# A hybrid mLSTM and attention layer on one core: the token's norm scale moves from x to the products of the projections

## What is computed

```
def rmsnorm(x, g):
    y = xf * lax.rsqrt(jnp.mean(xf * xf, axis=-1, keepdims=True) + EPS)
    return (y * g.astype(jnp.float32)).astype(x.dtype)
...
h = rmsnorm(x, g_pre_mix[l])
proj = h @ w_in[l]
m_qk, m_v, m_o, m_if, a_q, a_k, a_v, merge = jnp.split(proj, IN_SPLITS, axis=-1)
m_qk = jax.nn.silu(causal_dwconv(m_qk, m_conv_w[l], m_conv_b[l]))
...
hm = mlstm_chunkwise(..., i_pre, jax.nn.log_sigmoid(f_pre))
y_m = (jax.nn.sigmoid(m_o) * hm) @ w_branch_m[l]
ha = diff_attention(a_q, a_k, a_v, lam)
g_m, g_a = jnp.split(jax.nn.sigmoid(merge), 2, axis=-1)
mix = (g_m * y_m + g_a * y_a) @ w_out[l]
```

## Time and profile before

| | us |
|---|---|
| median of 3 runs | 1852.43 |
| lowest, highest | 1851.65, 1852.64 |
| span of the profiled execution | 1850.7 |
| TensorE busy | 1836.6 |
| VectorE busy | 1116.1 |
| ScalarE busy | 899.2 |
| first product of the projections starts | 12.72 |

### The profile page before, as it was taken

How to read it: one execution, slowest core, us unless ns; L and a number is a source line. 1 busy time by engine, 2 the same in 40 slices (tenths; PEclk the granted TensorE clock), 3 DMA queues, 4 the chain that set the end, 5 groups by cost and what they waited for, 6 DMA issues and landing times.

```text
span 1850.7 us, 35627 instructions
## 1 busy us (share of the span) xinstructions
PE 1836.6 (99%) x13864; PEld 1745.0 (94%) x13864; DVE 1116.1 (60%) x1340; ACT 899.2 (49%) x1174; POOL 66.6 (4%) x92
## 2 busy tenths in 40 slices
PE   8999999999999999999999999999999999999998
PEld 8999999999999999999999889999999999988886
DVE  6666556645665566545555557766667667755555
ACT  6554445444454455444434446555555555544443
POOL 2800000000000000000000000000000000000000
PEclk9999999999999999999999999999999999999999
DMA  7665666566656665666666754666666666665554
GB/s 241 194 192 175 191 182 177 177 188 181 178 172 192 179 176 177 188 193 193 192 192 196 253 198 149 194 193 194 193 193 193 192 194 190 196 215 193 194 193 143
DMA packets 164514, 351.44 MB, mean 190 GB/s; under 512 B 10937, under 2 KB 11473, under 8 KB 163793
## 3 DMA queue, kind: packets, MB, share of 16 engines
q1 hardware_dynamic: 162784, 344.11, 61.1%
q10 hardware_dynamic: 1280, 5.08, 0.7%
q0 software_dynamic: 368, 1.09, 0.2%
HBM read 348.12 MB, written 2.12 MB: 189 GB/s over the span
## 4 chain that ended last, share of the span: by engine, by line
PE 97%; issue 1%; DVE 1%; DMA 1%; ACT 0%; POOL 0%; DVEq 0%; POOLq 0%; SPq 0%; ACTq 0%
PE ps L1348 26%; PE ps L1347 26%; PE ps L1346 26%; PE ps L1563 11%; PE ps L1567 6%; PE ps L1523 1%; PE ps L1427 0%; PE ps L1499 0%; PE ps L1384 0%; DMA gm<-in_channel_rows 0%; DMA raw<-in_w_out 0%; PE ps L1500 0%; ACT ha_hi L631 0%; DVE x L926 0%; PE ps L1506 0%
## 5 line engine op out<-in xcount | busy, mean ns | idle before, releaser
L930 DVE TENSOR_TENSOR w_lo<-raw,w_hi 128x1024 fp32r<-128x1024 f32 x637 | 777.6, 1226 | 640.3 <-ACT w_hi L593 638.2
L593 ACT ACTIVATE w_hi<-raw 128x1024 fp32r<-128x1024 f32 (+1 forms) x641 | 677.7, 1060 | 767.1 <-PE ps L1348 606.9
L1346 PE MATMUL ps<-h,w_hi 128*128 128x256 f32 x3200 | 885.7, 277 | 0.2
L1348 PE MATMUL ps<-h,w_lo 128*128 128x256 f32 x3200 | 884.1, 276 | 0.0
L1347 PE MATMUL ps<-h,w_hi 128*128 128x256 f32 x3200 | 884.1, 276 | 0.0
L1346 PEld LDWEIGHTS ps<-h,w_hi 128*128 128x128 f32 x3200 | 600.9, 188 | 0.9 <-issue 0.6
L1347 PEld LDWEIGHTS ps<-h,w_hi 128*128 128x128 f32 x3200 | 600.8, 188 | 0.3
L1348 PEld LDWEIGHTS ps<-h,w_lo 128*128 128x128 f32 x3200 | 600.7, 188 | 0.0
L1563 PE MATMUL ps<-w_hi,ks_hi 128*128 128x512 f32 x448 | 174.5, 389 | 0.0
L1567 PE MATMUL ps<-w_lo,ks_hi 128*128 128x512 f32 x448 | 174.3, 389 | 0.0
L1563 PE MATMUL ps<-w_hi,ks_lo 128*128 128x512 f32 x448 | 138.1, 389 | 0.0
(11 more groups left out here) (180 smaller groups left out, 1432.4 us busy)
## 6 DMA issues: line engine op xcount, KB each, us to landing
raw<-in_w_in SPq DMA_DIRECT2D x287, 512.0 KB, 3.7
raw<-in_w_up SPq DMA_DIRECT2D x176, 512.0 KB, 4.4
raw<-in_w_down SPq DMA_DIRECT2D x88, 512.0 KB, 4.5
raw<-in_w_branch_m SPq DMA_DIRECT2D x32, 512.0 KB, 4.5
raw<-in_w_branch_a SPq DMA_DIRECT2D x32, 512.0 KB, 4.6
raw<-in_w_out SPq DMA_DIRECT2D x32, 512.0 KB, 4.7
x<-in_x ACTq DMA_DIRECT2D x1, 2048.0 KB, 12.5
gm<-in_channel_rows SPq DMA_DIRECT2D x2, 512.0 KB, 4.6
```

Source lines behind the costliest of these rows:

```text
L593: return nc.scalar.activation(out_ap, in_ap, ACT.Copy, scale=scale)
L930: nc.vector.tensor_tensor(w_lo[:, at:at + UNIT], raw[:, slot, :], w_hi[:, at:at + UNIT].bitcast(F32), ALU.subtract).then_inc(lo_done, 1)
L1346: nc.tensor.matmul(out_ap, stat_hi, mov_hi, start=start, stop=False, skip_group_check=True)
L1348: return nc.tensor.matmul(out_ap, stat_lo, mov_hi, start=False, stop=stop, skip_group_check=True)
```

## The change

x is laid out in DRAM by tiles of 128 columns and comes in five pieces, between the first weight units. It is transposed as it is, without the scale; `h_hi` and `h_lo` hold x times the gain. The squares, their sum and the root move into steps 2 to 8 of the first turn. The scale goes into a row (`rs_row`, the same on all partitions) through two small products (`scales_by_token`) that stand before unit 8. With it VectorE scales the products of six chunks in each turn, and of one per branch turn (`by_token`), and these steps replace ScalarE's copies; the tanh then reads SBUF. The conv reads a scaled copy in SBUF. The v chunks are scaled by partition, in two instructions each in place of one. The gates' 32 products stand before unit 8, `gate_rows` is now at u = 10 and `gate_exponents` at u = 11, and the gate rows take the scale and the bias on VectorE. The identity comes with the channel rows; the 18 identity transposes and six repeats are gone, and six products of a zero tile stand at the start. The table of the feed-forward's conv is loaded during the output projection.

```
-            for i in range(len(ROW_PIECES)):
-                sp.dma_start(row_piece(gm_rows, i), x_pieces[i]).then_inc(x_loaded[i], 16)
...
+            load_x(0)
             for k, done in ((0, first_loaded), (1, raw_loaded[0])):
                 sp.wait_ge(raw_free, 1)
                 sp.dma_start(raw[:, 0, k * 512:(k + 1) * 512], w_in_v[:, k, A_Q:A_Q + 512]).then_inc(done, 16)
+            for u in range(1, RING):
+                load_x(u)
+                load(BASE_MIX + u, u, chunk_unit(u, w_in_v, A_Q))
+            load_x(RING)
...
+            def row_squares(b, half):
...
+                nc.scalar.activation(ha_hi[:, k0:k0 + KT // 2, b * P:(b + 1) * P], gm[:, k0:k0 + KT // 2, b * P:(b + 1) * P],
+                                     ACT.Square, scale=float(D) ** -0.5,
+                                     accum_out=stat[:, X_MS + 2 * b + half:X_MS + 2 * b + half + 1]).then_inc(x_ms, 1)
...
+            scalar.wait_ge(chan_loaded, 16)
+            early_tile(0)
             scalar.wait_ge(first_loaded, 16)
             scalar.wait_ge(pe_done, 1)
             split_first(0, first_hi)
...
+            early_steps = {2: lambda: row_squares(0, 0), 3: lambda: row_squares(1, 0), 4: lambda: row_squares(0, 1),
+                           5: lambda: row_squares(1, 1), 6: wif_high, 9: scale_rows, 10: gate_rows}
...
-                    if u == 7:
                         scalar.wait_ge(pe_done, g * U_MIX + units_done(u))
-                        copy(qT[:], banks(0, 2, T)).then_inc(read_act, 1)
...
                         if t0 == 0:
-                            scalar.wait_ge(pe_done, g * U_MIX + units_done(u))
-                        conv_terms(g, c, c % 2, dst, (t0, t0 + 1))
+                            scalar.wait_ge(read_dve, g * 2 + (c - 2))
+                        conv_terms(g, c, dst, (t0, t0 + 1))
...
+            def repeat_scales():
...
+                    ins = nc.vector.tensor_scalar(rs_reps[:, b * P:(b + 1) * P], ident, 0.0, stat[:, X_RS + b:X_RS + b + 1],
+                                                  ALU.mult, ALU.add)
+                ins.then_inc(rs_rep, 1)
...
+            def by_token(out_ap, pair, done_unit, read):
+
+                vec.wait_ge(pe_done, done_unit)
+                nc.vector.tensor_tensor(out_ap, tiles_of(pair), rs_tiles, ALU.mult).then_inc(read, 1)
...
+                    if u == (10 if first else 7):
+                        by_token(qT[:], 0, g * U_MIX + units_done(7), read_qk)
...
-                    if u in (31, 33, 39, 41):
+                    if u in (31, 39):
+                        by_token(scaled, 1 if u == 31 else 0, g * U_MIX + units_done(u), read_dve)
+                    if u in (32, 33, 40, 41):
...
+            early_steps = {6: row_sums, 7: wif_parts, 8: repeat_scales, 9: lambda_dots, 10: rows_known, 12: lambda_full}
...
-            for i in range(18):
-                nc.tensor.transpose(ps[:, 0, 0:P], ident, ident)
...
+            def scales_by_token():
+
+                pe.wait_ge(rs_rep, 1)
+                for b in range(TB):
+                    last = nc.tensor.matmul(ps[:, 6, b * P:(b + 1) * P], rs_reps[:, b * P:(b + 1) * P], ident, start=True, stop=True)
+                last.then_inc(rs_psum, 1)
...
+                    if g == 0 and u == 8:
+                        scales_by_token()
+                        gates()
                     ready(g * U_MIX + (BASE_MIX + u))
```

More of the change, by code:

```diff
@@ L1431, in _ @@
             nc.tensor.sem_inc(pe_done, RING)
[L1433 to L1449 removed]
+            pe.wait_ge(zero_tile, 1)
@@ new lines, in _, with early_tiles @@
+            for i in range(6):
+                nc.tensor.matmul(ps[:, 0, 0:P], zeros, zeros, start=True, stop=True)
+            def early_tiles(pair):
+                for i in range(len(X_PIECES)):
+                    if X_PIECES[i][0] == 2 * pair:
+                        pe.wait_ge(x_loaded[i], 16)
+                for k in (2 * pair, 2 * pair + 1):
+                    for b in range(TB):
+                        ins = nc.tensor.transpose(early_place(k)[:, b * P:(b + 1) * P], gm[:, k, b * P:(b + 1) * P], ident)
+                    if ends_group(k):
+                        ins.then_inc(h_psum, 1)
@@ new lines, in first_products, with place @@
+            def first_products():
+                a_hi, a_lo = h_hi[:, 0, :], h_lo[:, 0, :]
+                def place(t):
+                    return ps[:, t // 2, t % 2 * T:t % 2 * T + T], slice(away(0) + t * P, away(0) + (t + 1) * P)
+                pe.wait_ge(first_hi, 1)
+                pe.wait_ge(h_hi_done, 1)
+                for t in range(4):
+                    out_ap, c = place(t)
+                    nc.tensor.matmul(out_ap, w_hi[:, c], a_hi, start=t % 2 == 0, stop=False, skip_group_check=True)
+                pe.wait_ge(h_done, 1)
+                for t in range(4):
+                    out_ap, c = place(t)
+                    nc.tensor.matmul(out_ap, w_hi[:, c], a_lo, start=False, stop=False, skip_group_check=True)
+                pe.wait_ge(first_lo, 1)
+                for t in range(4):
+                    out_ap, c = place(t)
+                    nc.tensor.matmul(out_ap, w_lo[:, c], a_hi, start=False, stop=False, skip_group_check=True)
@@ new lines, in gates @@
+            def gates():
+                pe.wait_ge(wif_ready, 1)
+                for k in range(KT):
+                    nc.tensor.matmul(ps[:, 7, 0:T], hm_hi[:, k, 0:P], h_hi[:, k, :], start=k == 0, stop=False,
+                                     skip_group_check=True)
+                    last = nc.tensor.matmul(ps[:, 7, 0:T], hm_hi[:, k, 0:P], h_lo[:, k, :], start=False, stop=k == KT - 1,
+                                            skip_group_check=True)
+                last.then_inc(gates_psum, 1)
```

346 lines of the change are left out of this document (192 added, 154 removed).

## The result

The changed kernel takes 1861.18 us (median of five runs, 1859.06 to 1861.94), the kernel before 1852.25 (1851.65 to 1852.64). The ratio is 1.0046, interval 1.0034 to 1.0058. The forecast was 1853.9 with a range to 1859.0: the time lies above it, and 7.3 us above the forecast. The profiled execution has a span of 1859.7 us against 1850.7.

What follows compares the result with a forecast made beforehand. TensorE was taken as the bound everywhere. The profiled 1850.7 us plus 1.1 for unit 8 starting later and 0.4 of waiting gave 1852.2; 1.7 for the runs made 1853.9, range 1848.5 to 1859.

Steps and rivals of the forecast that it cites:

- The first product: Start of the kernel: TensorE's first product at 7.9 us in place of 12.7, a gain of 4.8 us.
- To the end of unit 7: First turn: 7.9 + 22.0 for eight units + 3.3 for transposes + 2.0 for slow pace, ending at 35.2 us.
- The wait before unit 8: TensorE waits 2.9 us after unit 7 for both splits of unit 11, the two repeats and handing over.
- The scale and gate products: Before unit 8: 0.3 us for the new scale products and 3.7 us for the 32 gate products.
- the pace behind the wait: Rival: after the wait before unit 8 the next 4 us run at half pace, 2.0 us more, 1855.9; chance 0.15.
- GpSimd's start and chain: Gate chain on GpSimd starts 14.0 us after unit 8 starts and holds GpSimd for 53.66 us.
- the margin of 1.3: Unit 33: GpSimd's chain, root and VectorE's steps finish 1.3 us before TensorE wants the unit.
- The root for the attention heads: GpSimd's root behind the gate chain, ahead of VectorE's `on` and the split of unit 33: 2.1 us.
- GpSimd is late: Rival: GpSimd's chain runs slower beside VectorE and stops TensorE in unit 33; at 10%, 4.5 us, 1858.0; chance 0.13.
- the rest: Other copies changing engine cost 0, v chunks some tenths off the path, the feed-forward's table 0, at most 0.5 us.
- The conv in every turn: VectorE's chunk scaling before the conv, tight at u = 39 to 41: cost 0, holding by 0.5 us.
- The wait of 0.4 us at unit 37: First turn: VectorE's splits, scaling and conv taps come to 127.0 us against a need of 126.7; 0.4 us taken.

Runs made afterwards that it cites:

- the gates first: Changed kernel with one edit: before unit 8 TensorE runs the 32 gate products first and the two scale products second; 1856.91 us, 1.0024 against the kernel before.
- the run without the drain: Changed kernel with the drain in GpSimd's root for the attention heads replaced by a semaphore; 1856.05 us, 1.0019 against the kernel before.
- The kernel before with late gate rows: Kernel before with only the gate rows moved to steps 10 and 11 of the first turn and lambda to 12; 1853.74 us, 1.0008.
- the gates first and early: Changed kernel with gate products ahead of scale products, gate rows taken out in step 8 and exponents in step 9; 1849.93 us, 0.9987 against the kernel before.
- the root and unit 24 mended: Gates first and early, plus a semaphore for the root's drain and the attention-row transposes behind unit 25, not 24; 1850.08 us, 0.9990 against the kernel before.

## Why the prediction was wrong, step by step

**The first product** was put at 7.9 us and started at 7.02. The order of events was right: the table load waits for the first tile and starts at 4.68 us, as the row above has it. The channel rows with the identity landed near 3.9, not 5.0.

**To the end of unit 7:** 35.2 predicted, about 33.2 measured. 0.9 of the 2.0 us come from the earlier first product. The rest is the term for the slow pace, put at 2.0 us. The twelve first products, at 0.21 us each in place of 0.115, cost 1.2, and against the profiles with a fast start 0.7. That TensorE and not ScalarE is the later engine in this stretch was right.

**The wait before unit 8:** 2.9 predicted, 3.19 measured, by the very steps named. Right.

**The scale and gate products:** 4.0 predicted, 42.30 - 36.41 = 5.9 measured. The step that failed is the pace behind the wait. It stood among the rivals at 2.0 us and was left out of the sum; against the 4.3 us with the gates first it measured 1.6. The prediction held that the granted clock couldn't tell, since it read 1.00 in the slow start; behind this wait it does, with 0.50. Together with the 2.0 us by which unit 7 ended early this hid itself: unit 8 was put at 42.1 and started at 42.3, by two errors of some 2 us that cancel. That it hit was luck. The Trainium skill (TensorE: Matmul & The Clock Gate, Part 1: The HAM clock gate) says that the clock falls back when the array is idle, and that was the rule cited for this rival; behind the waits of 3.2 and 4.0 us the trace agrees, with products 0.21 us apart. Behind a wait of 3.18 us in another run it didn't happen, as the last section shows. Behind the wait of 1.0 us with the gates first it didn't happen: these products are 0.12 us apart.

**GpSimd's start and chain:** 56.1 and 53.7 us predicted, 57.03 and 54.8 measured. The step was 2 us short in sum, more than the margin of 1.3, and would have cost TensorE under 1 us by the prediction's own rule.

**The root for the attention heads** is the main failure. It was priced at 2.1 us, from one instance that came 12 us behind the last transfer, and took 7.3 us when it came straight behind it. The prediction moved GpSimd's chain up against the root and kept the root's duration. The row's idle time of 12.22 us was the hint that the two would meet. The margin of 1.3 us then became a wait of 4.0, and the wait brought 1.7 us of slow products. Sum 5.7 us, of 7.5 us missed in the span. With a root of 2.1 us, 5.2 less, the wait of 4.04 would not be there, the late chain included; the run without the drain shows that. The rival "GpSimd is late" had the engine, the place and the victim right, at 4.5 us, but by another mechanism (10% on the chain); the chain itself came out 2% longer.

**Unit 24:** the prediction put the attention's steps on VectorE at no cost, under "the rest", since each engine has three units of lead. It cost 1.45 us, and neither the place nor the mechanism (GpSimd's chain slowing VectorE's steps: 2.45 to 3.44 us, and 0.75 to 1.60) was in the sum or the rivals. The kernel before with late gate rows shows it without the rest of the change, 1.4 us.

**The conv in every turn:** put at 0, thin cover. TensorE's list shows no wait in turns 2 to 4, nor at units 37 and 45. Right, also the part that said that a wait there would falsify it. The wait of 0.4 us at unit 37 could not show, since TensorE had already stood at unit 33. Of the three signs that were to falsify the prediction (a wait in turns 2 to 4, no wait at unit 8, unit 8 more than 3 us off) none came, and the time was still outside the range: no sign was set on the root or on unit 24.

**The sum.** Against the predicted 1852.2 of span, the profile has 1859.7: 0.3 from the start of unit 8 (1.4 late where 1.1 was put), 1.45 at unit 24, 0.3 in small pieces up to unit 33, 4.04 of waiting there less the 0.4 foreseen, 1.7 of slow products, and +0.1 for the rest (0.6 up to the fourth turn's landmark, -0.5 at the end). That is 7.5.

## What to carry to other kernels

When a change moves a serial chain on a side engine, list what its next customer's step has ahead of it on that engine, transfers included, and price that step with them in flight; a duration read where the engine had been idle for 12 us can be too short, as 2.1 us was for 7.3. Where a small product waits for a result, put independent work of the same engine ahead of it: a TensorE wait of 3 us can be paid twice, once as time and once as pace. And a mark that comes out where it was put, as unit 8 did, confirms the sum behind it only if its terms are read one by one.

## What the runs showed of the hardware

- **A drain on GpSimd behind its own transfers** lasted until 0.5 us after the last of these had landed, in five kernels of five: gaps of 5.98, 5.91, 6.69, 5.62 and 5.48 us, against 0.83 with none in flight and 0.31 from the first to the second instruction with a semaphore in its place.
- **GpSimd's chain beside VectorE** stretches VectorE's two 128x1024 splits from 2.45 to 3.44 us and two 128x128 steps from 0.75 to 1.60; with GpSimd quiet the same program has 2.45 and 0.75. The Trainium skill (GPSIMD Engine Reference, 1. Specifications) says that GpSimd shares its SBUF interfaces with VectorE, and that VectorE's instructions with two SBUF inputs are among those that contend. The trace agrees: both stretched kinds have two tensor inputs in SBUF, and VectorE's 128x768 step just ahead of them, which has one of its two inputs in PSUM, takes 1.01 us before and 1.00 after. Not every such step is stretched: two 128x128 ones 5 us earlier take 0.75 in both.
- **The fall of the pace behind a wait isn't certain.** In the kernel with the semaphore in the root TensorE waited 3.18 us before the scale products, as long as after the change, and its gate products then ran at the upper level:

```profile
38.86 0.71 PE L1595 MATMUL ps<-chan,kT 128*128 128x128 f32 x4 [3.18 <-DVE kT L1094]
...
43.24 0.28 PE L1458 MATMUL ps<-h,w_hi 128*128 128x256 f32 x1
```

From the restart to unit 8 it took 43.24 - 38.86 = 4.4 us, against 5.9 after the change, and the granted clock reads 1.00 from 38 to 42 us. What decides whether the pace falls no run here shows. The scatter of the times doesn't settle it either: over ten runs it is 5.8 us with the gates first and the 4.1 us wait (1854.4 to 1860.3), 2.2 without the drain and with the 3.2 us wait, 1.1 with the gates first and early, and 2.6 with the root and unit 24 mended on top of it, the last two with no such wait.
